# Attention's prologue in the input map, group norms eight slots earlier, and GpSimd weighing two of four probability tiles

## The reference, cut to what matters

```python
kn, v = _expand_kv(ckv, w_ukv[l])
attn = _mla_attend(qn, qr, kn, kr, v)      # softmax(q k^T * scale) v
ret, sf, sb = _retention(rq, rk, rv, rg, logit_f, logit_b, s0_f, s0_b, gn)
...
lg = jax.nn.log_sigmoid(decay_logit)        # decay of each retention head
y = y_f + jnp.flip(y_b, 1)
mu = jnp.mean(y, axis=-1, keepdims=True)    # group norm over each head's 128 values
var = jnp.mean(jnp.square(y - mu), axis=-1, keepdims=True)
y = ((y - mu) * lax.rsqrt(var + EPS)) * gn
return jax.nn.silu(rg) * y, s_f, s_b
```

## Time and profile before

| | us |
|---|---|
| median of 3 runs | 2238.37 |
| range of these runs | 2236.64 to 2243.58 |
| the profiled execution | 2247.16 |
| its span | 2245.3 |
| mean granted clock of TensorE, share of full | 0.974 |

### The profile page before, as it was taken

One profiled execution on the slowest core, in us unless ns is written; L12 is line 12 of the kernel. 1 busy time (PEld: TensorE's weight loads), 2 busy tenths in 40 slices (PEclk: granted clock), 3 DMA queues, 4 the chain that ended last, 5 costly groups with the idle time before them and its releaser, 6 DMA issues. The chain is left out here.

```text
span 2245.3 us, 33445 instructions
## 1 busy us (share of the span) xinstructions
PE 2121.4 (94%) x12006; PEld 1166.2 (52%) x12006; DVE 1803.1 (80%) x3656; ACT 1246.4 (56%) x1678; POOL 433.7 (19%) x408
## 2 busy tenths in 40 slices
PE   6999996988789999999999999999999999999997
PEld 4667674555556754445555554544444444444443
DVE  4466636776777757889999999945899999999999
ACT  4555763455667635624444447768465565565562
POOL 0011110000111300223323232410223223223220
PEclk7999997998999999999999999999999999999998
DMA  7885751005667844778989998895888788788772
GB/s 293 329 312 162 224 203 57 29 19 216 215 207 263 303 159 159 240 252 261 355 303 341 319 355 310 324 370 220 334 298 322 292 300 319 292 302 321 291 276 75
DMA packets 193675, 573.86 MB, mean 256 GB/s; under 512 B 18784, under 2 KB 52352, under 8 KB 186368
## 3 DMA queue, kind: packets, MB, share of 16 engines
q1 hardware_dynamic: 113872, 323.99, 42.0%
q0 software_dynamic: 48704, 173.04, 20.7%
q10 hardware_dynamic: 30960, 75.07, 8.6%
HBM read 455.03 MB, written 117.00 MB: 255 GB/s over the span
## 5 line engine op out<-in xcount | busy, mean ns | idle before, releaser
L306 PE MATMUL mrg_ps<-h_hi,lin_hi 128*128 128x512 f16 (+1 forms) x1376 | 462.0, 359 | 2.8 <-DVE h_lo L639 2.8
L306 PE MATMUL mrg_ps<-h_lo,lin_hi 128*128 128x512 f16 (+1 forms) x1376 | 462.0, 359 | 0.0
L306 PE MATMUL mrg_ps<-h_hi,lin_lo 128*128 128x512 f16 (+1 forms) x1376 | 461.7, 358 | 0.0
L288 DVE SCALAR_TENSOR_TENSOR lin_lo<-lin_raw,lin_wsc,lin_hi 128x1024 f16<-128x1024 f32 x132 | 169.2, 1282 | 147.2 <-ACT lin_hi L282 147.0
L2074 POOL DMA_INDIRECT row<-v_dram,picked x128 | 177.8, 1389 | 558.3 <-DVE acc L2716 437.0
L2138 POOL DMA_INDIRECT row<-u_rows_dram,picked x128 | 176.1, 1376 | 472.0 <-DVE dot_junk L2324 354.0
L282 ACT ACTIVATE lin_hi<-lin_raw,lin_wsc 128x1024 f16<-128x1024 f32 x132 | 151.1, 1146 | 198.7 <-DVE lin_wsc L143 155.0
L2586 PE MATMUL ps_w<-oh_turned,oh_buf 128*128 128x128 f16 x1024 | 224.3, 219 | 5.4 <-ACT region L2252 5.3
L306 PEld LDWEIGHTS mrg_ps<-h_hi,lin_lo 128*128 128x128 f16 x1376 | 135.3, 98 | 128.2 <-issue 1.4
L306 PEld LDWEIGHTS mrg_ps<-h_hi,lin_hi 128*128 128x128 f16 x1376 | 134.4, 98 | 120.4 <-issue 4.1
L2824 PE MATMUL y_ps<-region 128*128 128x512 f16 x512 | 194.7, 380 | 1.8 <-PEq L2078 1.8
(11 more groups left out here) (424 smaller groups left out, 4007.5 us busy)
## 6 DMA issues: line engine op xcount, KB each, us to landing
lin_raw<-w_all_dram SPq DMA_DIRECT2D x132, 512.0 KB, 6.1
act_scratch<-activated ACTq DMA_DIRECT2D x128, 256.0 KB, 4.5
wgt_scratch<-region ACTq DMA_DIRECT2D x64, 512.0 KB, 6.4
region<-v_dram SPq DMA_DIRECT2D x15, 2048.0 KB, 7.7
oh_buf<-v_dram SPq DMA_DIRECT2D x15, 2048.0 KB, 7.6
act_buf<-w_all_dram SPq DMA_DIRECT2D x38, 512.0 KB, 4.7
lin_hi<-split_scratch SPq DMA_DIRECT2D x64, 256.0 KB, 3.3
lin_lo<-split_scratch SPq DMA_DIRECT2D x64, 256.0 KB, 4.8
```

Of the source, the lines that this page charges most:

```text
L288: nc.vector.scalar_tensor_tensor(out=self.lo[b][:], in0=self.raw[b][:], scalar=self.wsc[:, self.col(b)], in1=self.hi[b][:], op0=ALU.mult, ...
L306: last = nc.tensor.matmul(self.ps[b % 2][:, half, 0:ts.stop - ts.start], w_[:, kc, :], x_[:, kc, ts], start=(j == 0 and kc == 0), stop=(j ...
```

## The change

- Into the input map: VectorE begins the decay logarithm in slab 18 (two operations) and makes its series in slab 27; ScalarE takes its exponential in slab 20, ahead of the gates' Silu; TensorE makes the six groups of transposes in slabs 27 to 32 and VectorE evacuates them in slabs 28 to 33; the totals and their scales go to slabs 30 and 31; the scores of the context tokens to slabs 33 and 34, and their maxima to slab 35. SyncE loads `ksteps` in slab 26, not in the block of attention. `ps_n` is kept for both blocks, and is `pt` and `po` in the second.
- What stays of the prologue: the context's exponentials and weights, the first head's four tiles, the products with the context's values, the first decay table, the keys with their decays.
- Group norms: mean in slot 11 + 5h (k = 1), variance in 13 + 5h (k = 3), root in 14 + 5h, the five finishing operations in 15 + 5h (k = 0), the high half in 16 + 5h, the low half in 17 + 5h.
- GpSimd weighs the first two tiles (j = 0, 1) of units 1 to 7 as soon as VectorE's reciprocal is there; `turn_probs` of these units waits for GpSimd too.

```diff
 # input map, VectorE prepare(sl)
+if sl == 27:
+    decay_log()
+if 28 <= sl < 29 + NT:
+    k = sl - 28
+    dve.wait_ge(s("turned3"), k + 1)
+    nc.vector.tensor_copy(rv_tok[:, k, :] if k < NT else rk_tok, ps_n[:, k % 2, :]
+                          ).then_inc(s("turned3_read"), 1)
...
 # input map, ScalarE slab(q, b, left)
 if (q, b) == (gq, 0):
+    act.wait_ge(s("lg_abs"), 1)
+    nc.scalar.activation(lgw[:, 1, :], lgw[:, 0, :], ACT.Exp, scale=-1.0).then_inc(s("lg_exp"), 1)
     for h in range(RH):
...
 # input map, TensorE prepare(sl)
+if 27 <= sl < 28 + NT:
+    k = sl - 27
+    pe.wait_ge(s("v_read"), NALL // P)
+    if k >= 2:
+        pe.wait_ge(s("turned3_read"), k - 1)
+    for h in range(RH):
+        ...
+        last = nc.tensor.transpose(ps_n[:, k % 2, h * P:h * P + P], src, ident[:])
+    last.then_inc(s("turned3"), 1)
...
+if sl in (33, 34):
+    u = sl - 33
+    pe.wait_ge(s("turned3_read"), NT + u)
+    for k in range(4):
+        h = 4 * u + k
+        last = nc.tensor.matmul(ps_n[:, u, k * P:k * P + P], q_h[0:QK, h, 0:NCTX], k_h[0:QK, h, 0:NCTX],
+                                start=True, stop=True)
+    last.then_inc(s("ctx_scores"), 1)
...
 # attention: places of the group norms
-def var_head(u, k):
-    return u - CTX - 4 if k == 1 and 0 <= u - CTX - 4 < RH else None
-def mean_head(u, k):
-    return u - CTX - 3 if k == 4 and 0 <= u - CTX - 3 < RH else None
+def head_in(u, k, first):
+    h, late = divmod(5 * (u - CTX) + k - first, NT)
+    return h if late == 0 and 0 <= h < RH else None
+MEAN, VAR = 11, 13
...
 # attention, VectorE invert(u, j) and GpSimd
 V.reciprocal(rden[:, u, cs], den[:, u, cs]).then_inc(s("inverted"), 1)
+if by_pool(u, j):          # u > CTX and j < 2
+    return
...
+for u in range(CTX + 1, UNITS):
+    for j in (0, 1):
+        pool.wait_ge(s("inverted"), score_at(u, j) + 1)
+        nc.gpsimd.tensor_scalar(prob[u % 2][j], prob[u % 2][j], rden[:, u, j:j + 1], None, ALU.mult
+                                ).then_inc(s("pool_weighed"), 1)
...
 # attention, what is left of the prologue on VectorE
+maximum(CTX, 0)
+maximum(CTX, 1)
 invert(0)
 invert(1)
-maximum(CTX, 0)
-maximum(CTX, 1)
-for k in range(2, NT + 1):
-    turned(k)
 invert(CTX, 0)
 invert(CTX, 1)
...
 maximum(CTX, 2)
 maximum(CTX, 3)
 evacuate(1)
 invert(CTX, 2)
 invert(CTX, 3)
...
+dve.wait_ge(s("ret_ld"), 16 * 7)
 decay_logs(0)
...
```

More of the change, by code:

```diff
@@ L654, in build @@
                 ckv = sb(keep, "ckv", [P, NALL])
+                ps_n = pb(keep, "ps_n", [P, 2, 512])
+                CTX, UNITS = 2, 2 + HEADS
+                v_rest = v_flat[:, V_END:V_END + 2 * N]
+                small = v_flat[:, V_END + 2 * N:7 * N + PAST]
+                negmax, den, rden = (small[:, 4 * UNITS * k:4 * UNITS * (k + 1)].rearrange("p (u k) -> p u k", k=4) for k in range(3))
+                lgw = small[:, 12 * UNITS:12 * UNITS + 64].rearrange("p (w n) -> p w n", n=8)
+                lg = lgw[:, 7, :]
+                ksteps = small[:, 12 * UNITS + 64:12 * UNITS + 64 + 2 * RH]
+                rv_tok = proj[:, 0:4, :].rearrange("p k n -> p (k n)").rearrange("p (k n) -> p k n", k=NT)
+                rk_tok = ckv[:, 0:512]
                 q_h = x_t
@@ L1219, in score_at, with by_pool @@
                         return u if u < CTX else CTX + 4 * (u - CTX) + j
+                    def by_pool(u, j):
+                        return u > CTX and j < 2
                     def turn_at(u, k=0):
@@ L1354, in body @@
                                 lin.head(act, Q_UP, 0)
-                            if k == 3 and 0 <= h < RH:
-                                act.wait_ge(s("ret_scaled"), 1)
+                            if (h := head_in(u, k, VAR + 3)) is not None:
                                 act.wait_ge(s("ret_out"), h + 1)
@@ L1507, in body @@
                                 invert(u + 1, k - 1)
-                            h = u - CTX - 4
-                            if k == 1 and 0 <= h < RH:
+                            if (h := head_in(u, k, VAR)) is not None:
                                 dve.wait_ge(s("gn_var"), h + 1)
@@ L1528, in body @@
                                 low(u - 1)
-                            if k == 2 and 0 <= h < RH:
+                            if (h := head_in(u, k, VAR + 2)) is not None:
                                 dve.wait_ge(s("gn_root"), h + 1)
@@ L1538, in body @@
                                                 ).then_inc(s("ret_out"), 1)
-                            h = u - CTX - 3
-                            if k == 4 and 0 <= h < RH:
+                            if (h := head_in(u, k, MEAN)) is not None:
                                 dve.wait_ge(s("gn_mean"), h + 1)
@@ L1545, in body @@
                                                 ).then_inc(s("centred"), 1)
-                            h = u - CTX - 5
-                            if k == 0 and 0 <= h < RH:
+                            if (h := head_in(u, k, VAR + 4)) is not None:
                                 ret_low(h)
@@ L1666, in ret_values @@
                             last.then_inc(s("ret_av"), 1)
-                        score(0)
-                        score(1)
-                        turn(0)
-                        turn(1)
-                        score(CTX, 0)
-                        score(CTX, 1)
-                        for k in range(2, NT + 1):
-                            turn(k)
-                        score(CTX, 2)
-                        score(CTX, 3)
+                        for j in range(4):
+                            score(CTX, j)
                         turn_probs(0)
                         turn_probs(1)
-                        pe.wait_ge(s("exp"), CTX)
-                        nc.tensor.matmul(totals[:, 0:NALL // P], ones[:], hsum[:, 1, 0:NALL // P], start=True, stop=True
-                                         ).then_inc(s("att_total"), 1)
-                        total_pe(pe, "ret", totals[:, 8:8 + RH], 2, RH, "bound", 1)
-                        pe.wait_ge(s("att_scaled"), 1)
-                        pe.wait_ge(s("ret_scaled"), 1)
                         attend(0)
```

183 lines of the change are left out of this document (80 added, 103 removed).

## The result

The changed kernel takes 2249.93 us (median of 20 runs), the kernel before, measured beside it, 2242.78 (20 runs): a ratio of 1.0033, 95% interval 1.0024 to 1.0041, so slower by 0.33% or 7.2 us. The forecast was no change, 2238, with a range that ended at 2248. It was counted from the 2238.37 of the first three runs of the kernel before; of the 11.9 us between 2238 and 2249.93, 4.4 lie in that kernel's own median and not in the change.

The account below looks back on a forecast made before the run. TensorE was taken to bound units 1 to 4, VectorE to be fuller in prologue, unit 0 and from unit 5. Terms -13.8 + 5.4 + 6.1 + 2.0 = -0.3 us gave 2238, no change; own range 2232 to 2245, overall 2229 to 2248.

Parts of the forecast that it names:

- prologue and unit 0: Before unit 1: work leaving VectorE's queue lets unit 1 begin 13.8 us earlier, taken between 12.2 and 15.7.
- input map: Slabs taking over prologue work: TensorE 4.2 us, ScalarE's lateness 1.2; sum +5.4, ends 3.4 and 6.5.
- units 2, 3, 4 at the full clock: Earlier means and variances plus stalls behind finishing: +2.5, +4.1 and +2.6 us.
- half clock in units 3 and 4: Clock falling behind new stalls of about 3 us in units 3 to 5: +2.0 us, ends 0 and +6.
- units 5, 6, 7: Unit 5 a VectorE chain, square 15.0, variance 16.3: +1.7 us; units 6 and 7 lose norm work: -2.4 each.
- GpSimd: Weighings in units 1 to 7: twice VectorE's time each, nothing on the path, no gain beyond that already in sums.
- the 1.1 shorter of the one end nor the 3.5 late of the other: Unit 0: VectorE sheds two weighings, 1.1 us, gain 15.7; or TensorE's last slots at half clock, 3.5 later, gain 12.2.
- Stalls: Score of k = 2 waits for an exponential behind VectorE's finishing: some 2.6 us, 3.3 in even units.
- second rival: Half clock behind three stalls, 1.7 to 2 us each, unit 1 starting at half: +7.4 us, 2246; chance 0.25.
- first rival: Finishing operations do not stall TensorE; 11.3 us of stall and clock fall away: 2227; chance 0.17.
- third rival: GpSimd's 14 weighings each stop VectorE as long as they saved, 7.7 us: 2242 to 2245; chance 0.08.
- fourth rival: Prologue shrinks less than what left it, 4 us less gain: 2242; inside the forecast's chance of 0.50.

Follow-up runs that it names:

- e6: Changed kernel with four more TensorE matmuls ahead of the transposes in slots 17, 22 and 27, to fill the stalls; 2248.61 us, 1.0031 of the kernel before.
- e9: Changed kernel with 5, 6 and 7 filling matmuls ahead of the transposes of slots 17, 22 and 27; 2248.96 us, 1.0034 of the kernel before.
- e7: Changed kernel with group norms in their old slots and all weighings on VectorE, only the moved prologue left; 2234.60 us, 0.9965 of the kernel before.
- e10: Changed kernel with group norms in old slots, decay exponential behind slab 32's gate, all weighings on VectorE; 2232.43 us, 0.9956 of the kernel before.
- e3: Changed kernel with the finishing operations one slot later, in k = 1, and high and low halves following; 2251.63 us, 1.0036 of the kernel before.
- e8: Changed kernel with the finishing operations two slots later, in k = 2, mean and variance as changed; 2241.58 us, 1.0000 of the kernel before.
- e1: Changed kernel with the group norms back in their old slots, prologue and GpSimd as changed; 2235.04 us, 0.9969 of the kernel before.
- e2: Changed kernel with all weighings on VectorE again, none on GpSimd; 2252.28 us, 1.0051 of the kernel before.

## Why the prediction was wrong, point by point

| term, us | predicted | measured |
|---|---|---|
| prologue and unit 0 | -13.8 | -13.85 |
| input map | +5.4 | +6.5, with 1.7 of half clock |
| units 2, 3, 4 at the full clock | +9.2 | +8.4 (e6) |
| half clock in units 3 and 4 | part of +2.0 | +4.7 |
| units 5, 6, 7 | +1.7, -2.4, -2.4 | +3.9, -1.0, -2.6 |
| GpSimd | 0 | 0 to -4 |
| sum | -0.3 | +6 in the profile, +7.2 by medians |

- **Prologue.** Right. VectorE's first slot began 371.49 - 353.51 = 18.0 us after the block's start; 17.5 was forecast from its queue. From there to the end of unit 0 it took 16.9 us, before 16.6: neither the 1.1 shorter of the one end nor the 3.5 late of the other. The -13.8 was put between these ends without working of its own, but it holds: prologue and unit 0 take 34.55 to 35.21 us in the eleven other kernels, 34.85 in this one.
- **Stalls.** Right in place and nearly in size. The score of k = 2 waited 2.56 us in unit 3 for the named exponential (2.6 predicted). In unit 4 it was 2.93 (3.3 predicted), of which 1.94 stood ahead of the transposes, for VectorE's copy, and 0.99 at the score. Units 2 to 4 at the full clock, from e6 without the 1.0 that its filling added, are 67.8 - 59.4 = 8.4 longer than before.
- **The step that failed is the clock:** "I put +2.0 for that, ends 0 and +6", for the stalls of units 3 to 5. The half clock cost 1.7 in unit 3 and 3.0 in unit 4, 4.7 in these two alone, and unit 5 adds some 1.2. The 2.0 had no sum: it was put between unit 4 of the earlier trace rows (0.76 us idle, clock 1.00) and units 5 and 6 (5.07 idle, then a clock of 0.75). No full unit of the kernel before has a stall as long as the new ones, 2.56 and 2.93 us, behind which two thirds of that time and all of it were lost again.
- **Unit 5** is 2.2 over its forecast. Rows of slot 28 in the changed kernel, then one of e9, where the score of slot 27 ran at the full clock:

```profile
492.10 1.11 PE L1624 MATMUL ps_n<-ident,prob 128*128 128x128 f32 x4 [1.05 <-DVE lin_lo L1452]
493.01 2.34 PE L1602 MATMUL ps_s<-k_all,x_t 96*128 96x320 f32 x4
495.14 1.62 PE L1610 MATMUL ps_s<-act_buf,ckv 128*128 128x320 f32 x4
```

```profile
487.45 0.66 PE L1627 MATMUL ps_n<-ident,prob 128*128 128x128 f32 x4 [1.96 <-DVE lin_lo L1452]
```

  Slot 28 begins 13.72 us after the unit's start in both, set by VectorE's copy, so the slow score of slot 27 costs nothing. VectorE's low half, centring and copy ahead of the maximum, which the working does not name, make the square end 0.9 late (15.9 against 15.0). Then a score of 2.34 and a variance of 1.62, in place of 1.24 each, make the variance end 2.1 late (18.4 against 16.3). So of the 2.2 some 0.9 is VectorE's queue and some 1.2 half clock, an estimate from these rows.
- **Unit 6** is 1.4 over, at a clock of 0.82. One execution settles nothing here: e7 and e10, with the same work in the block of attention, took 18.58 and 20.20 in it, at 0.82 and 0.75. The prediction calls VectorE the fuller engine from unit 5 on and TensorE idle for a third of the time; in unit 6 of the earlier trace rows TensorE is busy 16.55 of 20.21 us and VectorE 14.35.
- **The map.** It is 1.1 over, and that too is the clock. TensorE's additions came to 3.8 in slabs 27 to 34, 4.2 predicted; the wait to 1.6, 1.2 predicted with 1.5 at most; what no term had was the half clock in slab 23, 1.67 (the other slabs were together some 0.5 shorter). In e3, e8 and e9, where the clock did not fall behind this wait, the map grew by 5.1 to 5.4.
- **The second rival came true** in its mechanism, half clock behind the stalls in full units, 1.7 and 3.0 us where it named 1.7 to 2. That its sum, +7.4, meets +7.2 is in part luck: it had -12.2 for the prologue, where -13.85 came, and 7 for three stalls that at 2 each make 6; the late start of unit 1 did not come. Of its sign, a clock below 0.9 in units 3 and 4, unit 4 showed 0.87 and unit 3 0.93. It had a chance of 0.25.
- **The first rival** (finishing finds cover) fell by the stalls; e8 shows the slot where it would have been right.
- **The third rival** fell by e1 and e2. Two decay tables were lengthened, beside GpSimd, by 0.39 us each (last section), but prologue and unit 0 took 34.56 us in e1 with GpSimd and 34.62 in e7 without.
- **The fourth rival** fell: the prologue shrank by what left it.

## What to carry to other kernels

Work that moves onto an engine with time to spare is paid by what stands behind it in that engine's queue: the same five operations cost 7.4 us more in one slot than two slots on, beside a long slot of the other engine. Price a new stall of 2 to 3 us in a stretch that is full by the stall and by the half clock behind it, here 1.7 and 3.0 us more, and take the price from rows with as long an idle time. An activation that needs another table brings its load along; here both stood on the path, 1.49 us, and moving them to where ScalarE idles made the map of the profiled execution 2.9 us shorter.

## What the runs showed of the hardware that was not expected

**A weighing on GpSimd** took 1.89 us, 3.4 times VectorE's 0.553, where the prediction had taken twice; no wait of TensorE was ended by it. It lengthened a VectorE operation beside it. The group of L1737 with the first and last start, then the timeline of the changed kernel, GpSimd and VectorE:

```profile
L1737 POOL TENSOR_SCALAR prob<-prob,v_flat x8: 1884/1886/2437, 376.1 to 512.5; 128x640 f32<-128x640 f32 x8
```

```profile
376.06 1.89 POOL L1737 TENSOR_SCALAR prob<-prob,v_flat 128x640 f32<-128x640 f32 x1 [48.55 <-DVE v_flat L1457]
...
376.25 1.53 DVE L1477 SCALAR_TENSOR_TENSOR lin_raw<-act_buf,v_flat 128x896 f32<-128x896 f32 x1
```

The decay table, an operation with two inputs in SBUF, took 1.53 us instead of 1.14 beside GpSimd; in e2, without GpSimd, all four took 1.14 to 1.15. The Trainium skill (SBUF — State Buffer, Summary: rules for kernel authors) says that a VectorE operation with two SBUF inputs contends with a GpSimd one that reads SBUF, and that the one that comes second is blocked until the first is done. The trace agrees with the first half and not with the second: blocked so, the table would have ended 1.14 after GpSimd's 377.95, and it ended at 377.78, before GpSimd. In the other order GpSimd is the one that is lengthened: its two weighings of 2.44 us began 0.18 behind a low half of VectorE (L1494, two inputs in SBUF), which kept its 0.87.

**The same wait, with and without a fall of the clock.** Nine of the kernels have the wait of about 1.9 us ahead of slab 23. In six of their profiled executions, the changed kernel's among them, slab 23 then took 9.9 to 10.0 at a clock of 0.83; in e3, e8 and e9 it took 8.24 to 8.27 at 1.00. So the fall behind a wait near 2 us comes in some executions and not in others; behind the stalls of slots 17 and 22 both executions that have them unfilled, the changed kernel and e2, showed it.
